# Six of eight heads' softmax factors go through DRAM scratch instead of a TensorE broadcast, and are applied three steps later

## What is computed

```python
logits = q_lat . c_sel * ATT_SCALE + bias          # per head, 512 queries x 512 keys at most
probs = softmax(logits)                            # over the selected, causal keys
o_lat = einsum('bqhk,bqkc->bqhc', probs, c_sel)    # 128 latent values per query and head
o = einsum('bshc,hcd->bshd', o_lat, w_uv)          # 64 values per query and head
```

## Time and profile before

| | |
|---|---|
| median of 3 runs | 1908.11 us (1906.39 to 1910.54) |
| profiled execution | 1911.47 us, span 1909.3 us |
| mean granted TensorE clock | 0.988 of full speed |
| busy: TensorE, VectorE, ScalarE, GpSimd | 96%, 57%, 35%, 9% of the span |
| sparse attention steps | from 1164 to 1256 us of the span |

### The profile page before, as it was taken

The page is one execution under the profiler, slowest core; times in us unless marked ns, Lnnn a source line. Parts: engine busy times, 40 slices in busy tenths (PEclk is TensorE's granted clock), DMA queues, the critical chain, the costliest instruction groups (busy, mean ns, idle before and its releaser), DMA issues.

```text
span 1909.3 us, 23744 instructions
## 1 busy us (share of the span) xinstructions
PE 1838.9 (96%) x8472; PEld 1487.4 (78%) x8472; DVE 1097.2 (57%) x1658; ACT 665.7 (35%) x1010; POOL 175.1 (9%) x125
## 2 busy tenths in 40 slices
PE   6999999999999999999999998999998999999989
PEld 4677888888888888888776766789776888888866
DVE  6565588887334655532253676587666655452265
ACT  5333333323323222222243334565453322222244
POOL 1221000000000000000022334433000000000000
PEclk9999999999999999999999999999999999999999
DMA  4677232223222222233211233232341322233211
GB/s 156 61 84 44 90 112 96 99 99 109 91 97 78 99 98 90 97 109 103 97 67 67 96 116 130 73 105 73 116 138 56 110 99 98 91 120 105 82 66 66
DMA packets 55460, 180.63 MB, mean 95 GB/s; under 512 B 6336, under 2 KB 7104, under 8 KB 55392
## 3 DMA queue, kind: packets, MB, share of 16 engines
q1 hardware_dynamic: 43344, 157.33, 24.6%
q10 hardware_dynamic: 12048, 22.40, 7.5%
HBM read 167.65 MB, written 12.06 MB: 94 GB/s over the span
## 4 chain that ended last, share of the span: by engine, by line
PE 82%; DVE 10%; DMA 3%; ACT 3%; issue 2%; ACTq 0%; POOL 0%; SPq 0%; DVEq 0%
PE bank L798 20%; PE bank L800 19%; PE bank L799 19%; PE bank L820 2%; PE bank L822 2%; PE bank L821 2%; DMA raw<-in_w_proj 2%; PE bank L894 2%; DVE score L2396 2%; PE bank L895 1%; PE bank L896 1%; DVE best L2395 1%; PE bank L836 1%; PE bank L869 1%; PE bank L1229 1%
## 5 line engine op out<-in xcount | busy, mean ns | idle before, releaser
L1338 ACT ACTIVATE w_hi<-raw 128x1024 fp32r<-128x1024 f32 (+2 forms) x281 | 304.5, 1087 | 734.7 <-PE bank L800 626.2
L798 PE MATMUL bank<-a_hi,w_hi 128*128 128x512 f32 x1192 | 467.4, 392 | 3.0 <-DVE gate L2380 2.4
L800 PE MATMUL bank<-a_hi,w_lo 128*128 128x512 f32 x1192 | 464.8, 390 | 0.0
L799 PE MATMUL bank<-a_lo,w_hi 128*128 128x512 f32 x1192 | 464.5, 390 | 0.0
L1954 DVE TENSOR_TENSOR w_lo<-raw,w_hi 128x1024 fp32r<-128x1024 f32 (+2 forms) x222 | 284.0, 1280 | 255.5 <-ACT w_hi L1338 242.2
L798 PEld LDWEIGHTS bank<-a_hi,w_hi 128*128 128x128 f32 x1192 | 224.2, 188 | 57.9 <-issue 8.0
L800 PEld LDWEIGHTS bank<-a_hi,w_lo 128*128 128x128 f32 x1192 | 224.1, 188 | 47.3
L799 PEld LDWEIGHTS bank<-a_lo,w_hi 128*128 128x128 f32 x1192 | 224.4, 188 | 46.1
L713 POOL TENSOR_TENSOR w_lo<-raw,w_hi 128x1024 fp32r<-128x1024 f32 x49 | 117.6, 2403 | 1056.1 <-ACT w_hi L1338 1056.1
L798 PE MATMUL bank<-h_hi,w_hi 128*128 128x512 f32 x528 | 205.4, 389 | 0.0
L799 PE MATMUL bank<-h_lo,w_hi 128*128 128x512 f32 x528 | 205.4, 389 | 0.0
(11 more groups left out here) (330 smaller groups left out, 2355.2 us busy)
## 6 DMA issues: line engine op xcount, KB each, us to landing
raw<-in_w_up SPq DMA_DIRECT2D x132, 512.0 KB, 3.4
raw<-in_w_down SPq DMA_DIRECT2D x48, 704.0 KB, 4.1
raw<-in_w_proj SPq DMA_DIRECT2D x59, 512.0 KB, 3.5
raw<-in_w_wo SPq DMA_DIRECT2D x8, 512.0 KB, 3.5
raw<-in_w_branch SPq DMA_DIRECT2D x16, 256.0 KB, 2.7
gates_in<-spill ACTq DMA_DIRECT2D x16, 256.0 KB, 2.9
raw<-in_w_out SPq DMA_DIRECT2D x8, 512.0 KB, 3.7
raw<-in_w_ple SPq DMA_DIRECT2D x8, 512.0 KB, 3.5
```

Of the source, the lines that this page charges most:

```text
L798: mm(dst[:, :], wh, hi[:, k, :], start=(first and c == 0), stop=False)
L799: mm(dst[:, :], wh, lo[:, k, :], start=False, stop=False)
L800: step = mm(dst[:, :], wl, hi[:, k, :], start=False, stop=(last and c == n - 1))
L1338: fn(w_hi[:, slot, 0:size], raw[:, slot, 0:size], ACT.Copy).then_inc(unit_high, 1)
```

## The change

For heads 0 to 5 the factors no longer go through TensorE and ScalarE. ScalarE issues, in step 4h+5, a store of the [128, 4] tile to one row of 512 numbers in DRAM scratch, element by element in token order, and in step 4h+7, after waiting for that store, a load of the row to all 128 partitions. The loads go to `rstd` and to `chunk[:, 1, :]` in turn. VectorE scales these heads in step 4h+10. The ya products of the first three pairs go to steps 15, 23 and 31. Heads 6 and 7 go the old way, at the old steps. The slot of `key_factors` is free again when the store has landed.

```diff
-YA_AT = {12: 0, 20: 1, 28: 2, DSA_STEPS + 3: 3}
+YA_AT = {15: 0, 23: 1, 31: 2, DSA_STEPS + 3: 3}
...
-            return QB * h + (7 if h < DSA_HEADS - 1 else 6)
+            return QB * h + (10 if h < DSA_HEADS - 2 else 7 if h < DSA_HEADS - 1 else 6)
+
+        by_dma = range(DSA_HEADS - 2)
+        factors = [rstd, chunk[:, 1, :]]
+
+        def factor_row(h):
+            return spill[27][h:h + 1, :]
...
-                    if i == QB - 1:
+                    if i == QB - 1 and h not in by_dma:
                         pe.wait_ge(sums_inverted, h + 1)
-                        if h:
-                            pe.wait_ge(factors_kept, h)
+                        if h - 1 not in by_dma:
+                            pe.wait_ge(factors_kept, 1)
...
-                if 3 <= a < DSA_STEPS + 3 and (a - 3) % QB == QB - 1:
+                for h in by_dma:
+                    if a == QB * h + 5:
+                        act.wait_ge(sums_inverted, h + 1)
+                        act.dma_start(factor_row(h).rearrange("h (j p) -> p (h j)", j=QB), key_factors(h),
+                                      allow_slow_non_contiguous=True).then_inc(factors_out, 16)
+                    if a == QB * h + 7:
+                        act.wait_ge(factors_out, 16 * (h + 1))
+                        if h >= 2:
+                            wait(tile_read("olat", h - 2))
+                        act.dma_start(factors[h % 2][:, :], factor_row(h).broadcast_to([P, T])).then_inc(
+                            factors_in[h % 2], 16)
+                if 3 <= a < DSA_STEPS + 3 and (a - 3) % QB == QB - 1 and (a - 3) // QB not in by_dma:
                     h = (a - 3) // QB
-                    act.wait_ge(factors_ready, h + 1)
-                    if h:
-                        wait(tile_read("olat", h - 1))
-                    fn(rstd[:, :], stat_bank[:, :], ACT.Copy).then_inc(factors_kept, 1)
+                    act.wait_ge(factors_ready, h + 1 - len(by_dma))
+                    wait(tile_read("olat", h - 2))
+                    fn(factors[h % 2][:, :], stat_bank[:, :], ACT.Copy).then_inc(factors_kept, 1)
...
                     if h >= 2:
-                        dve.wait_ge(factors_ready, h - 1)
+                        dve.wait_ge(factors_out, 16 * (h - 1))
                     v.reciprocal(key_factors(h), key_sums(h)).then_inc(sums_inverted, 1)
...
-                        dve.wait_ge(factors_kept, h + 1)
+                        if h in by_dma:
+                            dve.wait_ge(factors_in[h % 2], 16 * (h // 2 + 1))
+                        else:
+                            dve.wait_ge(factors_kept, h + 1 - len(by_dma))
...
-                        v.tensor_tensor(olat[:, h % 2, :], tile_bank("olat", h)[:, :], rstd[:, :],
+                        v.tensor_tensor(olat[:, h % 2, :], tile_bank("olat", h)[:, :], factors[h % 2][:, :],
                                         ALU.mult).then_inc(tile_sem("olat", h), 1)
```

More of the change, by code:

```diff
@@ L622, in two_blocks @@
         factors_kept = sem("factors_kept")
+        factors_out = sem("factors_out")
+        factors_in = [sem(f"factors_in{i}") for i in range(2)]
         hq_loaded = [sem(f"hq_loaded{i}") for i in range(2)]
```

## The result

| | before | after |
|---|---|---|
| median | 1909.45 us (6 runs, 1906.39 to 1911.59) | 1925.68 us (6 runs, 1924.16 to 1928.63) |
| ratio, with 95% interval | | 1.0088 [1.0078, 1.0098] |
| profiled execution | 1911.47 us, span 1909.3 | 1928.63 us, span 1926.5 |

The change costs 16.2 us. The forecast was 1903.9 and its range 1902 to 1909; what came is the last rival, the late store, to which it gave 0.12.

The account below looks back on a forecast made before the run. TensorE, busy 96% of the span, was taken as the bound. The terms -4.45 - 0.56 - 0.19 + 0.8 + 0.2 = -4.2 us took the median from 1908.11 to 1903.9 us; range 1902.0 to 1909.0.

Parts of the forecast that it names:

- the last rival: Store of factors lands late, ScalarE's wait holds attn_t: slower, +13 us at a 10 us landing; chance 0.12.
- I take 3.9 us: Landing time assumed for each head's 512-element store, if a 4-byte packet costs as much as a 2 KB one, 0.077 us.
- Both ends of the bound: Store's packet price: below, a 256 KB store at 0.077 us per packet; above, the bias-row store at 1.17 us.
- The budget: Store landing that ScalarE's wait tolerates without loss: about 7.8 us for heads 1 to 5, 3.1 us for head 0.
- The prediction's own line: Time change for a store landing x: 5(x - 7.8) + (x - 3.1) - 5.0, zero at x = 7.9 us.
- The gain of 4.45 us: TensorE loses the factor blocks of heads 1 to 5 in its fully busy stretch, 0.89 us each.
- The 0.8 us for its late store: Head 0's store queues behind the t_bias load, so ScalarE's wait delays attn_t for TensorE: 0.8 us lost.
- The waits of steps 29 and 33: Moving ya products removes TensorE's 0.56 us wait for an attention copy and 0.19 us wait for the last exponential.
- The forecast 0.2 us of head 5: Head 5's load, issued in step 27, delays attn_t of step 28 for TensorE: 0.2 us lost.

Follow-up runs that it names:

- the quarter of them: Changed kernel storing only the first factor column, 128 adjacent 4-byte elements, with the load reading an old row: 1911.84 us (one run) against 1908.83 before.
- the run with rows of 16 bytes: Changed kernel with each partition's four factors stored as one 16-byte element, VectorE reading the row in another order, same result: 1904.47 us against 1909.54 before.
- the moves alone: Changed kernel with all heads' factors still through TensorE and ScalarE; later scaling, two factor tiles and moved ya products kept: 1908.29 us against 1909.54 before.
- the run with the load that doesn't wait: Changed kernel with the same stores, but the load reads an old scratch row without waiting for the store: 1914.77 us, 1.0032 of before.

## Why the prediction was wrong

- **The step that failed** is the price of the store. "I take 3.9 us" was a price per packet at the DMA engines. As such it was right, even high: 528 packets of 4 bytes land in 3.0 us when they lie apart. But the landing was taken to end with the packets. At 16 single writes to each 64 bytes it comes 7 us after the last of them in heads 3 and 4, 9 us in head 1, and 10.8 us after the issue in the median. No run has the price of one packet by itself; what the runs show is that the packets ran in the same time at every distance. Both ends of the bound came from rows of packets as well, and so the range had no place for a cost that depends on addresses; the prediction named it only in half a sentence of a rival, "the 512 writes into one 2 KB row queue up at the memory".
- **That rival's two mechanisms** are told apart: a dear small packet ("a read and a write") is excluded as the cause by the elements 512 bytes apart, and crowded addresses are shown, by moving the elements. The number of writes is excluded as the main cause by the quarter of them. The Trainium skill, page "DMA: Bandwidth & Descriptors" (Specifications), says that the engine reads, modifies and writes below 512 bytes; if it does, that is part of the 3.0 us and no run separates it. The page's 10.5 ns per packet (Measured, for loads issued from GpSimd) gave an estimate of 5.5 us for 528 packets; the trace has 3.0 and 10.8 for the same packets. That one descriptor goes out for each element, as the page says (Rules for kernel authors), the trace confirms: the queue has (16080 - 12048) / 6 = 672 packets more per head, which is 512 + 128 and 16 for each of the two DMAs.
- **The budget was about right for heads 1 to 5, and wrong for head 0.** At a landing of 5.0 us (8 bytes apart) TensorE waits 0.3 us for attn_t, at 9.1 it waits 5.6, at 10.8 it waits 16.7. The prediction's own line gives 5 x 3.0 + 7.7 - 5.0 = +17.7 us at 10.8; +16.2 came. The agreement is luck. Its waits, 15 us for heads 1 to 5 and 7.7 for head 0, are 13.2 and 3.4 in the trace, 6 us too many. It leaves out two things that make up for them: the low clock after each standstill, and that the store holds up other transfers, which cost 11.4 us over the early store where nobody waits for it. At 9.1 us the same line gives +7.5, and the one execution with a quarter of the writes came out at +3.0. So the slope of the line isn't confirmed. Where the loss begins is about right: in that run the stores of heads 1 and 4 landed after 7.9 and 8.2 us and cost TensorE 0.4 and 0.7 us, though that of head 3 had landed, after 9.9, before ScalarE came to its wait.
- **The gain of 4.45 us** for five blocks is borne out where the store is early: 3.1 us of 3.6 between two scalings, 5.0 [3.2, 6.7] in the time.
- **Head 0.** The 0.8 us for its late store wasn't seen: in the run with rows of 16 bytes the store lands after 8.4 us and ScalarE waits 2.0 us for it, but TensorE waits for t_bias in that stretch anyway. Whether that wait grew by the block's 0.89 us isn't shown: it is 0.9 us before, 2.0 and 2.5 with elements 512 bytes apart and rows of 16 bytes, but 1.5 with the moves alone, where the block is still there, and 0.6 and none at 16 and 64 bytes.
- **Moves and head 5.** The waits of steps 29 and 33 went; their 0.75 us is below what the time can tell. The forecast 0.2 us of head 5 was 0.3, in the profile of every kernel with an early store.

**Still open:** what the memory does with the crowded writes. That they queue there, one behind another, would fit, but no row shows the inside of it, nor that it is the memory and not the way to it. It is not known either why the step from 8 to 16 is so much larger than the others: writes with no gap between them may be a case of their own. And whether 64 bytes are the size that matters is open; that piece is only a way to count the density here. Nor do the runs split the 11.4 us between loads that land late and the lower clock that follows.

## What to carry to other kernels

A transfer need not have landed when its packets have run: here up to 9 us lay between. A cost per packet from rows of large packets says nothing of many small ones with neighbouring addresses. Before storing a tile element by element, see whether the elements of a partition can go out as one piece and the reader take the other order: it was 128 packets for 512 and 3.5 us for 10.8. Where an in-order engine waits for a transfer, work out the landing at which it hurts. And don't count on hiding a slow store by waiting later: here taking the wait away brought back half of the loss, since the other half came from the transfers beside it.

## What the runs showed of the hardware

- 512 writes of 4 bytes without a gap land in 10.8 us, 128 such in 9.1; 8, 16, 64 and 512 bytes apart they land in 5.0, 4.3, 3.7 and 3.0.
- With adjacent elements, 8 bytes and 512 bytes alike, the packets of an undisturbed store (heads 3 and 4) have run 2.2 to 2.7 us after the issue. What follows them differs: 7 us, 1.7 to 2.6 us and 0.5 us until the landing.
- Such a store delays others in flight, on SyncE's queue too: in the run with the load that doesn't wait, weight units of 512 KB went from 3.5 to 7.5 us in the median, t_bias from 2.7 to 5.3.
- TensorE's clock at the start of the stage differs between executions of programs that are alike up to there (the kernels after and with the elements 512 bytes apart differ first in the store of step 5). Up to about 1164 TensorE stands still for the first exponential after the selection of keys. In the profiles before, after, of the load that doesn't wait and of 8 and 64 bytes this lasted 4.3 us, and the clock's mean from 1164 to 1170 was 0.50 to 0.67; in the other nine it lasted 3.1 us and the clock was 1.00. Why the standstill differs by 1.2 us is not known. Here after, and below with 512 bytes:

```profile
1164.00:1170.00 6.00, 5.53 (x16) 3.84 (x17) 3.62 (x9) 2.44 (x9) 2.91 (x4) 0.54 0.00 0
```

```profile
1164.00:1170.00 6.00, 6.00 (x35) 4.84 (x35) 4.18 (x13) 3.31 (x11) 3.41 (x4) 1.00 0.14 16
```

  16 matmul passes against 35 in 6 us: some 3 us of work. The three kernels with gaps that ran once fit it: 1904.84 and 1905.67 us with the low clock, 1901.28 without. That is of the size of the scatter between runs, and larger than most terms of the sum; whoever compares two single profiles over this stretch would put it down to the change.
